# Two transformer blocks on one core: norm sums by token on partitions, root and reciprocal of two values per partition, spread by TensorE

## What is computed

```python
def rms_norm(x, g):
    return x * lax.rsqrt(jnp.mean(x * x, axis=-1, keepdims=True) + EPS) * g

# first block
xn = rms_norm(x, attn_norm_g)                       # norm 0
proj = xn @ w_in                                    # attention q, k, v; gated linear attention q, k, v, r, gate
y_moba = attention(...)                             # 8 heads, causal, 256 keys
og = gla_attention(...)                             # 4 heads of 128 values
og = og * lax.rsqrt(jnp.mean(og * og, axis=-1, keepdims=True) + EPS) * gla_norm_g   # per head: the gated outputs
x = x + concat([y_moba, og * silu(gr)]) @ w_out     # mixer 1
hn = rms_norm(x, ffn_norm_g)                        # norm 1
x = x + (silu(h_gate) * h_val) @ w_ffn_down         # h = causal_dwconv(hn @ w_ffn_up)
x = rms_norm(x, final_norm_g)                       # norm 2
# second block: feed-forward (norm 3), mixer 2 (norms 4 and the latents'), feed-forward (norm 5), each modulated by c
return rms_norm(x, final_norm_2)                    # norm 6
```

## Time and profile before

| | |
|---|---|
| runs | 904.52, 901.42, 899.04 us; median 901.42 |
| profiled execution | 904.26 us, span 902.1 us |
| mean granted TensorE clock | 0.997 of full speed |
| busy: TensorE, its weight loads, VectorE, ScalarE, GpSimd | 97%, 94%, 79%, 53%, 10% |
| HBM traffic | 189.89 MB read and 1.05 MB written, 212 GB/s over the span |

### The profile page before, as it was taken

How to read it: one execution, slowest core, us unless ns; L and a number is a source line. 1 busy time by engine, 2 the same in 40 slices (tenths; PEclk the granted TensorE clock), 3 DMA queues, 4 the chain that set the end, 5 groups by cost and what they waited for, 6 DMA issues and landing times.

```text
span 902.1 us, 19304 instructions
## 1 busy us (share of the span) xinstructions
PE 877.0 (97%) x7302; PEld 845.7 (94%) x7302; DVE 709.4 (79%) x1108; ACT 476.0 (53%) x745; POOL 94.4 (10%) x141
## 2 busy tenths in 40 slices
PE   8999999999999999999999999999998999999996
PEld 5888898999999999999999999889998999999995
DVE  4898866889999779888887887979897988766443
ACT  4646574655554568344434565556545744444451
POOL 1031102000001320000001204000010200000000
PEclk9999999999999999999999999999999999999998
DMA  7453346556678985788889957755586478555641
GB/s 261 140 169 113 117 129 246 164 185 211 207 208 262 337 293 162 245 277 278 278 275 294 310 188 257 228 181 194 195 279 231 141 217 258 189 184 183 216 152 47
DMA packets 53334, 191.71 MB, mean 213 GB/s; under 512 B 5920, under 2 KB 6432, under 8 KB 53152
## 3 DMA queue, kind: packets, MB, share of 16 engines
q1 hardware_dynamic: 41760, 149.96, 50.6%
q0 software_dynamic: 10656, 39.33, 13.6%
q10 hardware_dynamic: 864, 1.67, 0.6%
HBM read 189.89 MB, written 1.05 MB: 212 GB/s over the span
## 4 chain that ended last, share of the span: by engine, by line
PE 84%; DVE 11%; ACT 3%; issue 1%; DMA 1%; SPq 0%; DVEq 0%; ACTq 0%
PE ps L394 25%; PE ps L395 25%; PE ps L396 25%; DVE w_lo L1240 4%; DVE ada_raw L1514 2%; ACT w_hi L848 1%; PE ps L468 1%; PE ps L470 1%; PE ps L469 1%; PE ps L561 1%; PE ps L504 1%; DMA raw<-w 1%; PE ps L535 1%; PE ps L475 1%; PE ps L401 0%
## 5 line engine op out<-in xcount | busy, mean ns | idle before, releaser
L1240 DVE TENSOR_TENSOR w_lo<-raw,w_hi 128x1024 fp32r<-128x1024 f32 x282 | 342.8, 1232 | 92.9 <-ACT w_hi L848 92.5
L394 PE MATMUL ps<-xh,w_hi 128*128 128x256 f32 x1296 | 366.6, 283 | 7.0 <-DVE w_lo L1240 4.6
L395 PE MATMUL ps<-xl,w_hi 128*128 128x256 f32 x1296 | 363.4, 280 | 0.0
L396 PE MATMUL ps<-xh,w_lo 128*128 128x256 f32 x1296 | 363.3, 280 | 0.0
L848 ACT ACTIVATE w_hi<-raw 128x1024 fp32r<-128x1024 f32 x282 | 288.3, 1052 | 46.7 <-PE ps L396 33.3
L394 PEld LDWEIGHTS ps<-xh,w_hi 128*128 128x128 f32 x1296 | 246.4, 190 | 11.1 <-issue 9.3
L396 PEld LDWEIGHTS ps<-xh,w_lo 128*128 128x128 f32 x1296 | 244.9, 189 | 0.0
L395 PEld LDWEIGHTS ps<-xl,w_hi 128*128 128x128 f32 x1296 | 243.4, 188 | 0.3 <-issue 0.2
L394 PE MATMUL ps<-act_hi,w_hi 128*128 128x256 f32 x528 | 147.8, 280 | 0.9 <-DVE w_lo L1240 0.9
L395 PE MATMUL ps<-act_lo,w_hi 128*128 128x256 f32 x528 | 147.6, 280 | 0.0
L396 PE MATMUL ps<-act_hi,w_lo 128*128 128x256 f32 x528 | 147.6, 280 | 0.0
(11 more groups left out here) (256 smaller groups left out, 1150.4 us busy)
## 6 DMA issues: line engine op xcount, KB each, us to landing
raw<-w SPq DMA_DIRECT2D x282, 512.0 KB, 4.4
ada_raw<-ada_w POOLq DMA_DIRECT2D x72, 512.0 KB, 4.8
X<-x_in SPq DMA_DIRECT2D x4, 256.0 KB, 5.8
bm<-bias_in POOLq DMA_DIRECT2D x1, 1024.0 KB, 6.9
out<-X SPq DMA_DIRECT2D x4, 256.0 KB, 2.4
tab<-tab_in ACTq DMA_DIRECT2D x1, 640.0 KB, 4.7
gmask<-gmask_in ACTq DMA_DIRECT2D x1, 512.0 KB, 5.6
cact<-c_in POOLq DMA_DIRECT2D x1, 512.0 KB, 6.3
```

The lines of the kernel that those rows point to most:

```text
L394: pe.matmul(o, lh, rh, start=start, stop=False, skip_group_check=True)
L395: pe.matmul(o, lh, rl, start=False, stop=False, skip_group_check=True)
L396: return pe.matmul(o, ll, rh, start=False, stop=stop, skip_group_check=True)
L1240: v.tensor_tensor(w_lo[:, slot(h), :], raw[:, slot(h), :], w_hi[:, slot(h), :].bitcast(F32), ALU.subtract).then_inc(lo_ready, 1)
```

## The change

- The sums of norms 0, 1 and 6 are taken the other way round (`token_sums`): a tile's squares are the weights, 128 tokens at a time, and one column of 1/1024 is the moving side. A norm's mean is then a 128x2 value, token on partition. Norm 0 sums its eight tiles this way, norm 1 tiles 0, 1, 6, 7 and norm 6 tiles 0, 7, each tile in two matmuls.
- Root (`root_tokens`) and reciprocal (`rstd_tokens`) work on 128x2. TensorE then spreads the result (`spread`, `norm_spread`): the 128x1 value, repeated along 128 columns, is the weights and the identity the moving side, so that every partition holds the 256 tokens' values, in PSUM bank 2. The products with `X` read them there. TensorE waits for the reciprocal before the spread, with the idle matmuls behind it; of these there are 2 now (`IDLE_SPREAD`) in the stages after norms 0 and 1.
- In norm 0 ScalarE takes the root between the two halves of the first chunk's `hi`, and VectorE takes the reciprocal between the two halves of its `lo`.
- The gated outputs get 8 such sums (4 heads x 2 groups of 128 tokens), a root and a reciprocal of 128x8, and 8 spreads of 128 columns in place of 4 of 256. `g_pick` and GpSimd's filling of it go.
- Output 7 of mixer 1 lies in bank 3 by itself. VectorE adds outputs 6 and 7 separately, 6 as soon as TensorE has completed it, and ScalarE squares them separately; `norm_tokens` waits for each square where it needs it.

```diff
 IDLE = 6
+IDLE_SPREAD = 2
...
-        def mix_out(o):
-
+        def mix_out(o, apart=False):
+
+            if apart and o == 7:
+                return ps[:, 3, 0:S]
             return ps[:, 4 + o // 2, (o % 2) * S:(o % 2) * S + S]
...
-                    keep_clock(u % 2, IDLE)
+                    keep_clock(u % 2, IDLE_SPREAD)
...
+            def token_sums(k, first, last):
+
+                for t in range(2):
+                    m = pe.matmul(ps[:, 2, t:t + 1], xn[:, k, t * P:t * P + P], mean[:, 0, 0:1], start=first and t == 0, stop=last, skip_group_check=True)
+                return m
+
+            def spread(o, src, start):
+
+                return pe.matmul(o, src.to_broadcast([P, P]), ident[:, :], start=start, stop=True, skip_group_check=True)
+
+            def norm_spread(n):
+
+                pe.wait_ge(rstd_done, n + 1)
+                for t in range(2):
+                    m = spread(ps[:, 2, t * P:t * P + P], rstd_t[:, t:t + 1], t == 0)
+                m.then_inc(rstd_spread, 1)
...
-                    m = ones(ps[:, 2, 0:S], xn[:, k, :], k == 0, k == KC - 1)
+                    m = token_sums(k, k == 0, k == KC - 1)
                 m.then_inc(ss_done, 1)
+                pe.wait_ge(consts_ready, 1)
+                norm_spread(0)
...
+            def norm_tokens(n, q, added, tiles_left):
+
+                pe.wait_ge(sq_sum, added)
+                for j, k in enumerate(tiles_left):
+                    if k >= 6:
+                        pe.wait_ge(sq_done, KC * q + k + 1)
+                    m = token_sums(k, j == 0, j == len(tiles_left) - 1)
+                m.then_inc(ss_done, 1)
+                norm_spread(n)
...
-                    m = three(mix_out(o), w_hi[:, slot(h), wc], w_lo[:, slot(h), wc], rh, rl, start and o % 2 == 0, False)
+                    m = three(mix_out(o, apart), w_hi[:, slot(h), wc], w_lo[:, slot(h), wc], rh, rl, start and (o % 2 == 0 or (apart and o == 7)), False)
...
-                            m = three(mix_out(o), w_hi[:, slot(h), wc], w_lo[:, slot(h), wc], ah[:, 4 + k, :], al[:, 4 + k, :], False, k == 3)
+                            m = three(mix_out(o, c == C_OUT1), w_hi[:, slot(h), wc], w_lo[:, slot(h), wc], ah[:, 4 + k, :], al[:, 4 + k, :], False, k == 3)
+                        if o == 6 and c == C_OUT1:
+                            m.then_inc(out6_full, 1)
...
-                        pe.wait_ge(go_sq, h // 2 + 1)
-                        m = pe.matmul(ps[32 * h:32 * h + 32, 2, 0:S], mean[:, 2, 0:32], b1["g_sd"][:, h, :], start=True, stop=True,
-                                      skip_group_check=True)
+                        pe.wait_ge(go_sq, 2)
+                        for t in range(2):
+                            m = pe.matmul(ps[:, 2, 2 * h + t:2 * h + t + 1], b1["g_sd"][:, h, t * P:t * P + P], mean[:, 2, 0:1],
+                                          start=h == 0 and t == 0, stop=True, skip_group_check=True)
                     m.then_inc(go_ss, 1)
...
-                    pe.wait_ge(pick_ready, 4)
                     pe.wait_ge(go_rstd, 1)
                     evacuated(pe, bank_use(10))
                     for h in range(4):
-                        m = pe.matmul(ps[:, 2 - 2 * (h // 2), (h % 2) * S:(h % 2) * S + S], b1["g_pick"][:, h, :], b1["g_rstd"][:, :],
-                                      start=h % 2 == 0, stop=True, skip_group_check=True)
+                        for t in range(2):
+                            o = (h % 2) * S + t * P
+                            m = spread(ps[:, 2 - 2 * (h // 2), o:o + P], b1["g_rstd"][:, 2 * h + t:2 * h + t + 1], h % 2 == 0 and t == 0)
...
-            norm_end(1, 2, (0, 1, 6, 7))
+            norm_tokens(1, 1, 2, (0, 1, 6, 7))
...
+            def root_tokens(n):
+
+                act.wait_ge(ss_done, n + 1)
+                f(sd[:, 0, 0:2], ps[:, 2, 0:2], ACT.Sqrt, bias=epsc[:, 0:1]).then_inc(sd_done, 1)
...
-            hi(0)
-            root(0)
+            hi(0, halves=(0,))
+            root_tokens(0)
+            hi(0, halves=(1,))
...
-                    f(b1["g_rstd"][:, :], ps[:, 2, 0:S], ACT.Sqrt, bias=epsc[:, 0:1]).then_inc(go_sd, 1)
+                    f(b1["g_rstd"][:, 0:8], ps[:, 2, 0:8], ACT.Sqrt, bias=epsc[:, 0:1]).then_inc(go_sd, 1)
...
-                square(1, 2 * j, 2)
                 if j < 3:
+                    square(1, 2 * j, 2)
                     hi(C_UP[0] + j // 2, halves=(j % 2,))
-            root(1)
+            square(1, 6)
+            square(1, 7)
+            root_tokens(1)
...
-            root(6)
+            root_tokens(6)
...
+            def rstd_tokens(n):
+
+                dve.wait_ge(sd_done, n + 1)
+                v.reciprocal(rstd_t[:, :], sd[:, 0, 0:2]).then_inc(rstd_done, 1)
...
-                rstd_of(n)
+                rstd_tokens(n)
+                if n == 0:
+                    lo(0, halves=(1,))
+                dve.wait_ge(rstd_spread, n + 1)
                 for j, (k0, n_) in enumerate(NEXT):
                     for k in range(k0, k0 + n_):
-                        ins = v.scalar_tensor_tensor(out=xn[:, k, :], in0=X[:, k, :], scalar=col(gain, k), in1=rstd[:, :], op0=ALU.mult, op1=ALU.mult)
+                        ins = v.scalar_tensor_tensor(out=xn[:, k, :], in0=X[:, k, :], scalar=col(gain, k), in1=ps[:, 2, 0:S], op0=ALU.mult, op1=ALU.mult)
...
-                rstd_of(n)
+                rstd_tokens(n)
+                dve.wait_ge(rstd_spread, 3)
                 for p in range(4):
                     dve.wait_ge(xg_done, 2 * p + 2)
-                    v.tensor_tensor(pair(X, p), pair(xg, p), over(rstd[:, :], 2), ALU.mult).then_inc(resid_done, 1)
+                    v.tensor_tensor(pair(X, p), pair(xg, p), over(ps[:, 2, 0:S], 2), ALU.mult).then_inc(resid_done, 1)
...
-                dve.wait_ge(half_used, 2 * c + 5 + j)
-                if gate is None:
+                if gate is not None or j < 3:
+                    dve.wait_ge(half_used, 2 * c + 5 + j)
+                if gate is None and j < 3:
                     v.tensor_tensor(pair(X, j), two(ps[:, 4 + j, :]), pair(X, j), ALU.add).then_inc(resid_done, 2)
                     return
                 for o in (2 * j, 2 * j + 1):
+                    if gate is None:
+                        if o == 6:
+                            dve.wait_ge(out6_full, 1)
+                        else:
+                            dve.wait_ge(half_used, 2 * c + 8)
+                        v.tensor_tensor(X[:, o, :], mix_out(o, True), X[:, o, :], ALU.add).then_inc(resid_done, 1)
+                        continue
...
-                    v.reciprocal(b1["g_rstd"][:, :], b1["g_rstd"][:, :]).then_inc(go_rstd, 1)
+                    v.reciprocal(b1["g_rstd"][:, 0:8], b1["g_rstd"][:, 0:8]).then_inc(go_rstd, 1)
```

More of the change, by code:

```diff
@@ L104, in build @@
         xl = sb("xl", [P, KC, S], F32R)
-        sb("on_line", [P, 78])
+        sb("on_line", [P, 76])
+        rstd_t = sb("rstd_t", [P, 2])
         rstd_w = sb("rstd_w", [P, SW])
@@ L315, in _ @@
             pool.memset(b1["AT1"][:, :, :], 0.0).then_inc(pool_zero, 1)
-            own.mark(pool.memset(b1["g_pick"][:, :, :], 0.0))
-            own.wait()
-            for h in range(4):
-                pool.memset(b1["g_pick"][32 * h:32 * h + 1, h, :], 1.0).then_inc(pick_ready, 1)
-            pool.wait_ge(pick_ready, 4)
             for l in range(LEVELS + 1):
@@ L576, in ffn_up, with mix_half @@
                         chunk(c0 + n + v, i=i)
-            def mix_half(h, rh, rl, start=False, ends_att=False):
+            def mix_half(h, rh, rl, start=False, ends_att=False, apart=False):
                 pe.wait_ge(lo_ready, h + 1)
@@ L702, in _ @@
             for k in range(4):
-                mix_half(2 * C_OUT1 + k, b1["yh1"][:, k, :], b1["yl1"][:, k, :], start=k == 0, ends_att=k == 0)
+                mix_half(2 * C_OUT1 + k, b1["yh1"][:, k, :], b1["yl1"][:, k, :], start=k == 0, ends_att=k == 0, apart=True)
                 if k == 0:
-                    pe.wait_ge(pick_ready, 4)
                     pe.wait_ge(go_rstd, 1)
@@ L1609, in _ @@
             dve.wait_ge(cols_landed, 16)
-            lo(0)
+            lo(0, halves=(0,))
             norm_plain(0, 0, "attn_g", 1)
```

7 lines of the change are left out of this document (4 added, 3 removed).

## The result

| | before | changed |
|---|---|---|
| runs, us | 904.52, 901.42, 899.04, 900.93 | 890.41, 890.07, 891.18, 889.62 |
| median | 901.17 | 890.24 |
| profiled execution (span) | 904.26 (902.1) | 890.41 (888.6) |
| mean granted TensorE clock | 0.997 | 0.991 |

The four places that the prediction priced turn out close to it. They hold only a fifth of the 13.85 us between the two profiled executions.

What follows compares the result with a forecast made beforehand. TensorE was taken as the bound, carrying 84% of what ended last. The terms -1.5 + 0.8 - 2.2 - 1.6 = -4.5 us, from the median 901.42 us, gave 896.9 us; range 894.0 to 902.0.

Steps and rivals of the forecast that it cites:

- four places: Start, gated outputs in mixer 1, norm after mixer 1 and last norm; together -4.5 us.
- start: First norm: small reciprocal between VectorE's two splits, first product at 13.9 instead of 15.42; gain 1.5 us.
- gated outputs: Mixer 1: 16 one-column passes instead of 8 on four column groups; 1.2 us lost, 0.44 regained, loss 0.8.
- norm after mixer 1: Shorter sums, root and reciprocal, with the bank split; TensorE goes on at 147.0; gain 2.2 us.
- last norm: Kernel's end: four passes left after the last square, spread to 895.05 against a product at 896.61; gain 1.55 us.
- Clock rivals: Granted clock falls to half at the start (898.8 us, chance 0.18), or after mixer 1 too (901.0 us, chance 0.08).
- Slower by passes in series: Load and product of each one-column pass stand in series, 0.35 us a pass: +10.8 us, 912 us, chance 0.07.
- Head start absorbed: Modulation transfers from mixer 1's end delay a weight half, losing up to 2.2 us: 899.1 us, chance 0.05.
- first clock rival: Clock falls at the start, whose gain becomes nothing or a loss up to 1 us: 898.8 us, chance 0.18.

Runs made afterwards that it cites:

- b_xr32: Kernel before with only the two buffers of the shifted input (xr_h, xr_l) 32 bytes further: 893.52 us, ratio 0.9872.
- a_xr0: Changed kernel with only the two buffers of the shifted input moved back 32 bytes to where the kernel before has them: 901.56 us, ratio 0.9951.
- b_pad32: Kernel before with 32 bytes of unused SBUF space per partition, moving every buffer behind it to its place in the changed kernel: 897.23 us, ratio 0.9919.
- c_gla: c_best with the norm of the gated outputs in mixer 1 as in the kernel before: 887.28 us, ratio 0.984.
- d_gla: As c_gla but without any extra idle products: 886.26 us, ratio 0.9814.
- a_clk: Changed kernel with dense idle products between one-column sums at the start and between sums and spread in the first two norms: 889.25 us, ratio 0.9847.
- a_nopad: Changed kernel with its 128x2 values kept in the statistics buffer, so buffers behind it lie as in the kernel before: 901.65 us, ratio 0.9967.
- c_small: c_best with the idle products between the groups of sums at the start 128 instead of 256 columns wide, three of them: 888.30 us, ratio 0.9856.
- a_again: Changed kernel, unchanged, run once more: 892.52 us (one run).
- c_best: Changed kernel with idle products, buffers as in the kernel before except the two of the shifted input 32 bytes further: 888.60 us, ratio 0.9843.

## Why the prediction was wrong

**The step that failed** is the premise: "Between these places everything waits for something issued a little before, so I carry a shift through to the end unchanged." The stream between the places did not keep its pace. Loops 2 and 3 gave 3.8 us each, because xr moved by 32 bytes (b_xr32, a_xr0: shown). Loop 1 gave 4.2 (cause not shown). Between loops 2 and 3 the products on xr and on xh gave 0.8, the 0.5 on xh again by xr's position. The three down stages took back 0.5, 0.3 and 0.3; b_pad32 shows the last as an effect of moving buffers alone. The output halves of mixer 1 took 0.9. I had priced the instructions that the change adds and removes, and not the two lines of the diff that change where buffers lie (the statistics buffer cut from 78 to 76 columns, `rstd_t` added behind it). No rival covered this, so the range could not either.

A second step failed with it: the clock, which the forecast put at nothing. It cost 0.8 at the start and 1.2 after mixer 1, which accounts for the four places having given 2.7 instead of 4.5.

**The steps by their own terms** (us, minus is a gain):

| step | predicted | measured, two traces |
|---|---|---|
| start | -1.5, with the clock fall 0 to +1 | -0.6: VectorE's chain gained 1.46 (15.42 to 13.96), the first dense product 1.25; the fall cost 0.6 more |
| gated outputs | +0.8 | +0.7; +0.64 by c_gla and by d_gla. Not in the sum: 0.8 behind it, in the output halves |
| norm after mixer 1 | -2.2, with the clock fall 0 | -1.2: the first dense product came 2.4 nearer to mixer 1, the fall then cost 1.2 |
| last norm | -1.55 | -1.6 |
| sum | -4.5 | -2.7 |

- *Prices.* Reciprocal 0.18, measured 0.163. Root 0.20, measured 0.26. Spread 0.70, measured 0.71. One-column passes: 16 in 1.95, less the first load and last tail, over 15 gaps: 0.112, with 0.11 forecast. The Trainium skill, "TensorE: Matmul & The Clock Gate", section "LDWEIGHTS (loading the stationary operand)", gives 128 columns at 1.2 per ns as an estimate of 0.107; the trace agrees to 0.005.
- *Clock rivals:* right in kind (0.50 at both places), too dear. I charged 1.9 at the start and 2.2 more after mixer 1; the traces show 0.8 (0.2 ahead of the first dense product, 0.6 behind it) and 1.2, and a_clk, whose clock did not fall, got back 1.1 for both.
  I gave them 0.18 and 0.08, too little: without extra idle products all seven traces show the fall at the start, and four of the seven the one at the norm. At the start dense work was away for 6.2 us, longer than the 4.2 ahead of the fall in the earlier trace rows, and I still counted one-column passes as likely to hold the clock.
- *Slower by passes in series:* excluded by 0.112. *Head start absorbed:* no such wait; the shift went through.

Without the moved buffers the change is a_nopad: ratio 0.9967, on the 901.17 us of the result 898.2 us (896.3 to 900.1). That is inside the range and near the 898.8 of the first clock rival. In part this is luck: a_nopad's start gained 1.5 in spite of a fall of the clock, and its output halves lost 0.8 that no term held.

## What to carry to other kernels

A change of buffers is a change of layout: before pricing instructions, compare the addresses of all operands in the two built kernels, and where they moved, keep a version in which they have not. In a stream that is 100% busy, count passes per stretch at the same clock; a pace 4% off over a third of the kernel outweighs every wait that a page of the profile shows. And look at the products ahead of a stretch as well as at its own operands: 32 bytes in their position, or another form of them, changed its pace here. Before a difference of 1 to 5 us between two traces is put down to an edit, look whether the clock fell in one of them alone, and take a second trace of the same kernel.

## What the runs showed of the hardware

- Dense 256-column fp32r passes with a 128-column load each have two paces that last for whole stages at 2.4 GHz, 512 or 532 in 60 us (0.1177 and 0.1133 us from start to start). The Trainium skill, "TensorE: Matmul & The Clock Gate", section "Back-to-back issue gap", would give 256 / 2.4 + 2.5 = 109 ns as an estimate for an isolated one. No run here shows that.
- Which pace a stretch has does not depend on its own code and operands alone: it can be set by 32 bytes in the position of the operands of the products ahead of it (532 instead of 512 in b_xr32, back to 511 in a_xr0), and goes with the form of the work ahead of it (109 or 104 passes in 12 us, c_gla and c_small). Why is not settled.
- The granted clock can fall at the same place in one trace of a kernel and not in the next: 0.79 over 142 to 150 us in the changed kernel, 1.00 in a_again. Idle products do not make it certain either: up to 114 us TensorE has the same work in c_best and c_gla, the granted clock is 0.50 and 1.00 at 12 to 14 us, and the first dense product of c_best comes 2.7 us later (17.99 and 15.28).
